# Two merges with their first gates computed in the periods before them, the first FFN sums copied, and the bias transfers of the attention spread

## The reference

```python
gate_a = jax.nn.sigmoid(proj[..., C_GA:C_GB]).astype(x.dtype)
gate_b = jax.nn.sigmoid(proj[..., C_GB:IN_COLS]).astype(x.dtype)
merged = (gate_a * jnp.einsum('bsc,cd->bsd', o_a, w_branch_a[l])
          + gate_b * jnp.einsum('bsc,cd->bsd', o_b, w_branch_b[l]))
y = jnp.einsum('bsd,de->bse', merged, w_out[l])
```

```python
g_a, g_b = jnp.split(jax.nn.sigmoid(gate_logits + b_gate[l]), 2, axis=-1)
x = x + (g_a * y_a + g_b * y_b) @ w_out[l]
```

## Time and profile before

| | us |
|---|---|
| median of 3 runs | 2591.44 (2588.71 to 2592.77) |
| profiled execution | 2593.04 |
| its span (first to last instruction) | 2591.2 |
| PE busy, of the span | 2259.7 (87%) |
| DVE / ACT / POOL busy | 1075.1 / 762.9 / 884.6 |

### The profile page before, as it was taken

The page is one execution under the profiler, slowest core; times in us unless marked ns, Lnnn a source line. Parts: engine busy times, 40 slices in busy tenths (PEclk is TensorE's granted clock), DMA queues, the critical chain, the costliest instruction groups (busy, mean ns, idle before and its releaser), DMA issues. The chain is left out here.

```text
span 2591.2 us, 30368 instructions
## 1 busy us (share of the span) xinstructions
PE 2259.7 (87%) x11615; PEld 1756.5 (68%) x11615; DVE 1075.1 (41%) x1752; ACT 762.9 (29%) x1195; POOL 884.6 (34%) x789
## 2 busy tenths in 40 slices
PE   6999888888768988999996997889998899499994
PEld 4888767777656877788884665678887687344441
DVE  3122346666733145433335554455664435301112
ACT  4333243333314224222214444312121323011110
POOL 3433156565525452444421102335432443000001
PEclk8999899999979998999997999889998899599998
DMA  5323023222114413333213312111101323779994
GB/s 170 90 74 84 18 79 83 76 59 70 37 23 108 112 57 130 114 97 95 94 54 77 70 57 78 26 30 29 21 5 41 106 82 125 294 317 419 419 418 185
DMA packets 284280, 292.95 MB, mean 113 GB/s; under 512 B 77712, under 2 KB 247952, under 8 KB 274512
## 3 DMA queue, kind: packets, MB, share of 16 engines
q1 hardware_dynamic: 275416, 259.45, 31.8%
q0 software_dynamic: 5280, 19.18, 2.1%
q10 hardware_dynamic: 3456, 12.58, 1.2%
HBM read 318.33 MB, written 23.17 MB: 132 GB/s over the span
## 5 line engine op out<-in xcount | busy, mean ns | idle before, releaser
L2271 PE MATMUL moe_bank<-ex_wgu,Y 128*64 128x512 f32 x768 | 172.3, 600 | 3.2 <-DMA ex_wgu<-in_w_up_e 1.6
L2271 PEld LDWEIGHTS moe_bank<-ex_wgu,Y 128*64 128x64 f32 x768 | 66.6, 139 | 103.6 <-issue 103.6
L2243 POOL DMA_INDIRECT hT<-token_rows,rows x24 | 22.8, 951 | 315.9 <-PE moe_bank L2256 237.5
L667 PE MATMUL gdn_bank<-hh,gdn_ws 128*128 128x512 f32 x256 | 116.1, 454 | 8.1 <-POOL gdn_ws L846 8.1
L667 PE MATMUL m_bank<-hh,m_wgs 128*128 128x512 f32 x256 | 101.7, 397 | 18.1 <-POOL m_wgs L1458 18.1
L1458 POOL TENSOR_TENSOR m_wgs<-hT,m_wgs 128x1024 fp32r<-128x1024 f32 x32 | 80.5, 2517 | 96.9 <-ACT m_wgs L1497 96.9
L1551 DVE TENSOR_TENSOR X<-X,m_bank 128x512 f32<-128x512 f32 x32 | 22.0, 688 | 210.4 <-PE m_bank L669 210.4
L667 PE MATMUL ff_bank<-ff_wds,ff_hes 128*128 128x512 f32 x256 | 100.8, 394 | 4.7 <-DVE Y L1973 4.7
L1973 DVE TENSOR_TENSOR Y<-Y,ff_bank 128x512 f32<-128x512 f32 x128 | 84.4, 685 | 47.2 <-PE ff_bank L669 47.2
L846 POOL TENSOR_TENSOR gdn_ws<-gdn_wr,gdn_ws 128x1024 fp32r<-128x1024 f32 x30 | 71.2, 2378 | 95.2 <-ACT gdn_ws L1126 95.2
L669 PE MATMUL gdn_bank<-hh,gdn_ws 128*128 128x512 f32 x256 | 102.8, 402 | 0.0
(11 more groups left out here) (569 smaller groups left out, 6125.0 us busy)
## 6 DMA issues: line engine op xcount, KB each, us to landing
ex_wgu<-in_w_gate_e SPq DMA_DIRECT2D x48, 1024.0 KB, 16.9
ex_wgu<-in_w_up_e SPq DMA_DIRECT2D x48, 1024.0 KB, 19.7
ex_wd<-in_w_down_e SPq DMA_DIRECT2D x48, 1024.0 KB, 22.0
Y<-in_w_in SPq DMA_DIRECT2D x48, 512.0 KB, 4.0
hT<-in_w_in SPq DMA_DIRECT2D x34, 512.0 KB, 4.2
wu<-in_w_ff SPq DMA_DIRECT2D x16, 1024.0 KB, 12.4
ff_wd<-in_w_ff SPq DMA_DIRECT2D x16, 1024.0 KB
gdn_wr<-in_w_in SPq DMA_DIRECT2D x30, 512.0 KB, 4.0
```

Source lines behind the costliest of these rows:

```text
L667: pe.matmul(bank, left(0, l), right(0, r), start=(start and n == 0), stop=False)
L2243: pool.indirect_dma_start(hg[:, j, :], None, rows_dram, bass.IndirectOffsetOnAxis(rows[:, pair_of[q]:pair_of[q] + 1], 0)).then_inc(h_in[j] ...
L2271: ins = pe.matmul(bank[2 + j][half, :], hgT[:, j, k, half], w[:, e, k], start=(k == 0), stop=(k == KT - 1))
```

## The change

Four edits, of which the first is the large one.

1. In both recurrences four gate blocks (q = 0 and 1, both gates) are appended to the projections: prepared from the last projected head's period on, multiplied between the products of the last period, and passed through the sigmoid by ACT into a free part of `G.X`. The merges then start with `ready = 2`: their first products are the branches of q = 0, and after the branches of q PE makes the gates of q + 2. The early loads at the end of the recurrence bring the first branch block instead of two gate blocks. In `m2` the bias is read in place instead of through a copy made by DVE. The rooms that buffers have in `G.X` and `G.hT` are chosen anew.
2. `ff`: no memset; the first group's sums are copied from PSUM instead of added.
3. Attention, POOL: the bias lines go out after r = 4 instead of r = 3, and the four transfers back are issued one each after r = 5 to 8.
4. Attention, ACT: `high(1)` comes after the third of the eight copies of the input instead of after the eighth.

```diff
@@ attention_phase, POOL
-                if r == 3:
+                if r == 4:
                     pool.wait_ge(s.lines_ready, 3)
                     pool.dma_start(lines_dram, lines).then_inc(s.lines_out, 16)
-                    pool.wait_ge(s.lines_out, 16)
-                    for h in range(DHG):
...
+                if 5 <= r < 5 + DHG:
+                    if r == 5:
+                        pool.wait_ge(s.lines_out, 16)
+                    h = r - 5
...
@@ attention_phase, ACT
-            high(1)
+                if k == 2:
+                    high(1)
@@ gdn_phase, SP (blocks 32 to 35 are the gates'; nblocks = 4 * GH + 4)
+            load(4 * GH + 2)
+            load(4 * GH + 3)
@@ gdn_phase, POOL
                 if g is not None:
                     lower(4 * g + 1)
+                elif p == GH - 2:
+                    lower(4 * GH + 1)
+                elif p == GH - 1:
+                    lower(4 * GH + 2)
+                    lower(4 * GH + 3)
@@ gdn_phase, PE
                 i, h, g = stages(p)
+                if p == GH - 1:
+                    g = GH
@@ gdn_phase, ACT
+            def gate(u):
+                act.wait_ge(s.proj, 4 * GH + u + 1)
+                act.activation(gates[:, u], bank[u % 2][:, :], ACT.Sigmoid).then_inc(s.gs, 1)
...
+                if p == GH - 1:
+                    gate(0)
+                    higher(4 * GH + 2)
+                    gate(1)
+                    take_u(i, 0)
+                    higher(4 * GH + 3)
+                    take_u(i, 1)
...
+                if p == GH - 1:
+                    gate(2)
+                    gate(3)
@@ merge_phase, PE
+            for q in range(ready, 2):
+                gates(q)
             for q in range(KT):
...
-                for n in range(2):
-                    pe.wait_ge(s.gate_l, 2 * q + n + 1)
...
+                if q + 2 < KT:
+                    gates(q + 2)
@@ merge_phase, ACT
+            high_a(0)
             for k in range(4):
                 split(k)
-            high_gate(0, 0)
-            high_gate(0, 1)
-            high_branch(0)
+            high_b(0)
             for k in range(4, ka + kb):
                 split(k)
@@ ffn_phase, DVE
-            dve.memset(G.Y[:], 0.0).then_inc(s.zero, 1)
-            dve.wait_ge(s.zero, 1)
...
+                    if isinstance(i, int) and i == 0 and j == 0:
+                        dve.tensor_copy(y, bank[4 + o % 4][:, :]).then_inc(s.added, 1)
+                        continue
@@ rwkv_phase, POOL (blocks 15 to 18 are the gates')
                 if g is not None:
                     lower(3 * g + 6)
+                else:
+                    lower(nblocks - 2)
                 if i is not None:
                     mask_b(i, 2)
+                if g is None:
+                    lower(nblocks - 1)
@@ rwkv_phase, PE, last period: 16 steps in the levels, then
                         keys(i, st)
+                        if g is None:
+                            fill(2)
                         states(i, st)
                         outputs(i, st)
+                        if g is None:
+                            fill(1)
...
+                if g is None:
+                    fill(2)
@@ rwkv_phase, ACT, last period
+                if g is None:
+                    higher(nblocks - 2)
+                    act.wait_ge(s.yz, 6 * PAIR)
+                    gate(0)
...
+                        if g is None and st == 0:
+                            higher(nblocks - 1)
+                            gate(1)
```

More of the change, by code:

```diff
@@ L739, in gdn_phase @@
         wab, first = gdn_early(G)
-        raw = [first[0], first[1]] + [wr[:, r % 2] for r in range(2, 4 * GH)]
+        nblocks = 4 * GH + 4
+        raw = [first[0], first[1]] + [wr[:, r % 2] for r in range(2, nblocks)]
+        gates = G.X[:].rearrange("p a b -> p (a b)")[:, 0:4 * T].rearrange("p (u t) -> p u t", u=4)
         ab = spare[:, 256:384].rearrange("p (t c) -> p t c", t=NT)
@@ L1445, in _ @@
+            for q in range(ready, 2):
+                load_gates(q)
+                if q == 0:
+                    load_branches(0)
+            if ready:
+                load_branches(0)
+            if gate_bias is not None:
+                sp.dma_start(gb[:], gate_bias).then_inc(s.bias_in, 16)
+            for q in range(KT):
+                if q + 2 < KT:
+                    load_gates(q + 2)
+                if q + 1 < KT:
+                    load_branches(q + 1)
             for k in range(2):
@@ L1506, in high_branch, with high_b, sigmoids @@
+            def high_b(q):
+                act.wait_ge(b_ready[q % 2], 16 * (q // 2) + 16)
                 if q:
                     act.wait_ge(s.b_mm, q)
-                act.activation(wbs[:, 0], wb[:, j], ACT.Copy).then_inc(s.b_h, 1)
+                act.activation(wbs[:, 0], wb[:, q % 2], ACT.Copy).then_inc(s.b_h, 1)
             def split(k):
                 act.activation(oh[:, k, :], branch[k], ACT.Copy).then_inc(s.o_h, 1)
+            def sigmoids(q):
+                if q >= 2:
+                    act.wait_ge(s.mixed, q - 1)
+                for n in range(2):
+                    act.wait_ge(s.gate_mm, unit(q, n) + 1)
+                    act.activation(sg[:, q % 2, n, :], bank[4 * (q % 2) + 2 + n][:, :], ACT.Sigmoid,
+                                   bias=gb[:, q, n:n + 1] if gate_bias is not None else 0.0).then_inc(s.sig, 1)
@@ L1532, in _ @@
[L1532 to L1533 removed]
+                    high_a(q + 1)
+                    high_b(q + 1)
+                if q + 2 < KT:
+                    sigmoids(q + 2)
         @block.vector
@@ L3323, in rates, with gate @@
                     act.activation(kd[:, d, :], af[:, d, g, :], ACT.Identity, bias=par[:, g, 5:6], scale=par[:, g, 1:2]).then_inc(s.ar, 1)
+            def gate(u):
+                act.wait_ge(s.proj, first_gate + u + 1)
+                act.activation(gates[:, u], bank[(first_gate + u) % 2][:, :], ACT.Sigmoid, bias=gb[:, u // 2, u % 2:u % 2 + 1]).then_inc(s.gs, 1)
             def take(g, t):
```

226 lines of the change are left out of this document (133 added, 93 removed).

## The result

The kernel with the change takes 2563.05 us (median of 4 runs, 2561.7 to 2571.54) against 2592.11 before: a ratio of 0.9898, 95% interval 0.9882 to 0.9913, so 1.0% faster. Timed once more with the experiments it took 2566.78 (5 runs, ratio 0.9894, 0.9875 to 0.9913); all nine runs together have their median at 2563.9, 28 us under before, where 24.9 were forecast. Its profiled execution took 2561.7 with a span of 2559.9, 31.3 less than before.

What follows compares the result with a forecast made beforehand. PE work was taken to bound the merges' body, while in the recurrences' last periods PE waits, partly at half clock. Terms -7.2 (attention), -4.6 (`gdn` with `m1`), -13.1 (`rw` with `m2`), 0 (`ff`): -24.9, so 2567 us; range 2557 to 2582.

Steps and rivals of the forecast that it cites:

- Attention: Attention, bias transfers: PE's 5.88 us wait before r = 4 goes, 0.8 us lost at r = 7; -7.2 us, bounds -5.9 and -8.2.
- `gdn`, period 6: `gdn`, start of period 6: block 33's `lower` slows DVE's decays, delaying the inverse and period 7; +1.7 us.
- `gdn`, period 7: `gdn`'s last period: 32 gate steps, 21.7 us of work, lengthen the chain by 6.2 us; its end adds 2.5.
- `m1`: First merge: four gate blocks fewer, -21.7 us, but block 0 bound by DVE's splits; 145.1 against 160.1, -15.0 us.
- the last is ready 19 us after the phase's start: `m1`, block 0: about five of DVE's twelve splits held by POOL subtractions, block 0 ending at 20.0 us; bounds 14 and 24.
- `rw` and `m2`: `rw`'s period 3: chain +7.1 us, tail +0.2; `m2` 117.8 instead of 138.2 us, -20.4; net -13.1.
- `ff`: `ff`: dropping the memset and copying the first sums from PSUM changes nothing; 0 us, bounds 0 and -1.
- late preparation: Rival, last periods: late gate weights hold PE's chain, about 3 us for each of four blocks; 2579 us, chance 0.18.
- Half clock: Rival, last periods: gate steps run at half clock, 64 steps costing 0.60 us more each; 2605 us, chance 0.04.
- The attention's wait: Rival, attention: the wait stays because spread issues make r = 5 to 8 late in turn; 2573 us, chance 0.06.
- Everything warm: Rival, merges: splits mostly free, full clock kept, block 0 ends 5 us sooner in `m1`, 2 in `m2`; 2558, chance 0.12.
- The drain of a table load: Before the last norms: the skill's about 1.38 us extra per table load, left out of the sum; with it 2570 us.

## Why the prediction was right

The likeliest case was the one that came, 2567 forecast and 2563.05 measured, and the range held it. By its own steps:

1. **Attention.** Right: no gap from c = 2 to c = 3, and what was named as late next is late: 0.96 us before r = 7 at 63.03, where 0.8 were forecast. -6.9 by the medians, -6.6 in the profile, for -7.2. The scatter of both (299.0 to 303.2 us where the stage is changed) is larger than what is left between them and the forecast.
2. **`gdn`, period 6.** The decays took 3.78 us (before 2.18) beside a subtraction of 2.35, as forecast. The period, counted to the arrival of the inverse, took 46.8 us instead of 45.6: 1.2 for 1.7.
3. **`gdn`, period 7.** From its first product to the chain's last 40.7 us, where it took 35.0: +5.7 for +6.2. A state step is 5.0 for 5.3. The end cost what was said: a step, the sigmoid and 1.28 us of table load, and the square 0.01 us after it. Sum of items 2 and 3 +9.4 for +10.4.
4. **`m1`.** Here it is a matter of which execution one looks at. The step "the last is ready 19 us after the phase's start" rested on splits that are held by POOL. In the executions in which DVE and POOL take turns the mechanism is the forecast one: five splits are held, the last is done 18.5 us after the start, and `m1` takes 153.2 to 154.6 us, 14 to 15 less than before's 168.65, for -15.0. With `gdn`'s +9.4 that is about -4.7 for -4.6, and the medians give 6.4. In the profile above no split of the b-branch is held, block 0 ends 15.6 us after the start, near the lower bound of 14, and the gain is 20.7. The late weights of q = 7 cost 1.05 us for 1.0.
5. **`rw` and `m2`.** The net was nearly right (-13.4 us by the table, for -13.1), the parts were not: `rw`'s last period from its first product to the last write takes 60.6 us where it took 51.3, +9.3 where 7.3 were forecast, and `m2` -24.3 where 20.4 were. In `rw` the chain was nearly right: 49.1 us for 48.6, where it took 41.5. The term that failed is the tail behind it, +1.8 (from 9.7 to 11.5 us) for +0.2. The forecast counted one table load there, and the rows above show two, 2.56 us, the second between two activations that followed each other at once before; PE waits 1.59 us for the activation behind the first of them (0.78 before, behind no load). At the end of `gdn` there is one, because ACT there loads a table set that serves both activations (`natural_log_exp_and_others`, L1187), which the tail of `rw` does not. No run takes `rw`'s loads away, so that they make up the whole 1.6 us is argued, not shown. In `m2` block 0 ended 11.5 us after the start for 13.7 and 1.0 of half clock: its eight splits took 3.15 and 3.20 us together, since POOL's gate blocks came after them. Medians: moving `m2`'s gates 12.5 us; the 13.1 of the forecast holds the order too. That the two misses, +2.0 and -3.9, have opposite signs is luck, and it brings the sum nearer to the measurement than its parts are.
6. **`ff`.** From `o1`'s first product to `ff`'s last 417.4 and 417.5: 0, as forecast.

The rivals: no gap in the last periods is ended by POOL ahead of a gate step, so late preparation is out. Half clock is out, 0.90 and 1.00. The attention's wait did not stay. "Everything warm" is half true: in the first profile block 0 ends 4.4 us sooner than the sum has it in `m1` and 2.2 in `m2`, which are near that rival's 5 and 2, because the splits were free; but the products at the start ran at half clock, and the clock there is worth at most 0.9 us, as the products ahead of them show. The drain of a table load did not show: in each of the three loads shown above the next activation starts 0.01 us behind it.

What stays open: who gets through where a split and a subtraction meet. And `ff`'s copied sums were never run alone; that they are worth nothing is read from the stage's 417.4 and 417.5 us.

## What to carry to other kernels

A chain whose engine waits at half clock is the place for matmuls that stand in a full stage, as long as they fit its gaps: 32 steps, 21.7 us of work, cost 3.5 to 6 us there, and the whole 21.7 behind the chain; once the engine is busy throughout, as in `rw`'s last period (47.9 of 49.1 us), there is nothing left to hide more behind, and four steps moved in `gdn` gained about 1 us at most. Count each table load that a sigmoid put ahead of a norm causes: the end of `gdn` has one, the end of `rw` two. When two engines' elementwise work meets at the start of a phase, let the less urgent one wait for the other with a semaphore, so that the order is yours; here that cost nothing in the stage (147.89 us against 147.94, in the profile where DVE kept the lead). And compare stages over several profiles before a difference of a few us is explained: here unchanged stages differ by 2 to 5 us.

## What was not expected of the hardware

- The same instructions at the same distances gave two outcomes, 6.5 us apart: POOL's subtraction of 128x1024 took 5.17 us while DVE ran on through its splits of 128x512 at 0.60 us each, or 2.74, with the next splits at up to 2.88. The Trainium skill, "SBUF — State Buffer", section "SBUF: two separate sides", says that of such a pair (DVE with two inputs in SBUF, and GpSimd) the one that starts first has the shared ports for its whole instruction and the other blocks. The single instructions agree (2.88 us beside 2.83 and 2.74); but in the first outcome POOL's subtraction, begun at 796.77, was passed by four DVE splits that began after it (from 797.19), which that rule does not give.
- Stages that the change does not touch differ between executions: from `o1`'s first product to `rw`'s first it took 628.8 us before and 628.1 to 631.3 in the others, and in `rw`'s third period the same 48 matmuls run at full clock in the kernel with POOL's wait (from 261.9 to 267.4 us after `rw`'s first product) and at half clock in the changed one (262.9 to 272.3); the half clock there stands in two of the thirteen profiles. The chain of `gdn`'s last head without gate steps took 35.0 or 35.1 us in three profiles and 37.0 to 37.2 in three. The +1.8 us after `o1` and 1.6 of `rw`'s +10.9 in the table above are of this kind: no edit is known to cause them.
